# Two long-convolution stages: convolution taps of two tiles in turn, narrow sums in four column tiles, layer-norm statistics per token, other places for the z units

## The reference, cut to what matters

```python
def conformer_conv_mixer(h, w_in, conv_w, conv_b, ln_g, ln_b, w_out):
    proj = h @ w_in                                  # 1024 -> 3 x 2048
    val, glu_gate, z = jnp.split(proj, 3, axis=-1)
    u = val * jax.nn.sigmoid(glu_gate)
    u = causal_depthwise_conv(u, conv_w) + conv_b    # 31 taps per channel
    u = jax.nn.silu(layer_norm(u, ln_g, ln_b))       # over the 2048 channels
    return (u * jax.nn.silu(z)) @ w_out              # 2048 -> 1024
```

## Time and profile before

| | us |
|---|---|
| three runs | 1513.99, 1516.18, 1511.05 (median 1513.99) |
| profiled execution | 1511.99 |
| its span in the profile | 1510.0 |
| PE busy | 1485.9 |
| DVE, ACT, POOL busy | 1044.5, 828.2, 500.1 |

### The profile page before, as it was taken

One profiled execution on the slowest core, in us unless ns is written; L12 is line 12 of the kernel. 1 busy time (PEld: TensorE's weight loads), 2 busy tenths in 40 slices (PEclk: granted clock), 3 DMA queues, 4 the chain that ended last, 5 costly groups with the idle time before them and its releaser, 6 DMA issues.

```text
span 1510.0 us, 26643 instructions
## 1 busy us (share of the span) xinstructions
PE 1485.9 (98%) x10179; PEld 1372.2 (91%) x10179; DVE 1044.5 (69%) x2139; ACT 828.2 (55%) x1522; POOL 500.1 (33%) x459
## 2 busy tenths in 40 slices
PE   8999999999999999999999999999999999999999
PEld 6888899998899999999988888989888878999987
DVE  6899967455777786666599997666247667775532
ACT  4576656445665544444456676555336655555442
POOL 2687643433334200000057785154421112000033
PEclk9999999999999999999999999999999999999999
DMA  7554365666654568866444444654843223576653
GB/s 216 146 153 140 123 197 168 222 172 152 128 151 154 153 189 208 209 179 195 141 140 140 140 140 158 192 142 131 214 153 95 74 84 113 168 206 185 169 187 118
DMA packets 308114, 239.49 MB, mean 159 GB/s; under 512 B 18017, under 2 KB 286707, under 8 KB 307988
## 3 DMA queue, kind: packets, MB, share of 16 engines
q1 hardware_dynamic: 295816, 228.70, 52.0%
q10 hardware_dynamic: 12172, 9.10, 2.6%
HBM read 236.02 MB, written 1.75 MB: 157 GB/s over the span
## 4 chain that ended last, share of the span: by engine, by line
PE 80%; DVE 13%; ACT 3%; DMA 1%; issue 1%; POOL 1%; SPq 0%; DVEq 0%; ACTq 0%; POOLq 0%
PE bank L782 16%; PE bank L784 8%; PE bank L785 7%; PE bank L786 7%; PE bank L835 3%; DVE bank L1117 3%; PE bank L837 3%; PE bank L836 3%; PE bank L1633 3%; PE bank L1635 3%; PE bank L1634 3%; PE bank L1260 2%; DVE wlo L379 2%; PE bank L798 2%; PE bank L761 1%; PE bank L762 1%
## 5 line engine op out<-in xcount | busy, mean ns | idle before, releaser
L379 POOL TENSOR_TENSOR wlo<-ring,whi 128x1024 fp32r<-128x1024 f32 x101 | 252.5, 2507 | 852.1 <-ACT whi L370 852.1
L370 ACT CAST whi<-ring 128x1024 fp32r<-128x1024 f32 x330 | 339.3, 1046 | 228.0 <-PE bank L786 79.9
L379 DVE TENSOR_TENSOR wlo<-ring,whi 128x1024 fp32r<-128x1024 f32 (+1 forms) x229 | 294.1, 1294 | 186.9 <-ACT whi L370 185.9
L782 PE MATMUL bank<-sqb,ring 128*128 128x256 f32 x1504 | 330.3, 379 | 0.9 <-DMA ring<-in_a_w_in_dram 0.9
L782 PEld LDWEIGHTS bank<-sqb,ring 128*128 128x128 f32 x1504 | 285.4, 190 | 41.2 <-DMA ring<-in_a_w_in_dram 1.3
L784 PE MATMUL bank<-xh,whi 128*128 128x256 f32 x928 | 264.7, 285 | 1.5 <-DVE xl L707 1.5
L785 PE MATMUL bank<-xl,whi 128*128 128x256 f32 x928 | 263.2, 284 | 0.0
L786 PE MATMUL bank<-xh,wlo 128*128 128x256 f32 x928 | 263.1, 284 | 0.0
L1054 POOL TENSOR_TENSOR scratch<-scratch 128x256 f32<-128x256 f32 x288 | 200.3, 731 | 106.0 <-ACT scratch L999 95.3
L1117 DVE SCALAR_TENSOR_TENSOR bank<-scratch,convw,bank 128x256 f32<-128x256 f32 x576 | 231.1, 482 | 0.0
L784 PEld LDWEIGHTS bank<-xh,whi 128*128 128x128 f32 x928 | 178.7, 193 | 4.6 <-issue 3.5
(11 more groups left out here) (312 smaller groups left out, 2746.0 us busy)
## 6 DMA issues: line engine op xcount, KB each, us to landing
ring<-in_a_w_in_dram SPq DMA_DIRECT2D x64, 512.0 KB, 5.2
ring<-in_b_w_in_dram SPq DMA_DIRECT2D x32, 1024.0 KB, 6.0
ring<-in_c_w_in_dram SPq DMA_DIRECT2D x64, 512.0 KB, 5.4
ring<-in_w_in_dram SPq DMA_DIRECT2D x26, 1024.0 KB, 5.3
ring<-in_w_ffn_in_dram SPq DMA_DIRECT2D x44, 512.0 KB, 5.1
ring<-in_a_w_in_dram SPq DMA_DIRECT2D x16, 1024.0 KB, 5.2
ring<-in_a_w_out_dram SPq DMA_DIRECT2D x16, 1024.0 KB, 5.3
ring<-in_w_ffn_out_dram SPq DMA_DIRECT2D x10, 1024.0 KB, 5.0
```

The lines of the kernel that those rows point to most:

```text
L370: nc.scalar.copy(piece(whi, h)[:, :, 0:n], src).then_inc(hi_done, 1)
L379: engine.tensor_tensor(piece(wlo, h)[:, :, 0:n], src, piece(whi, h)[:, :, 0:n].bitcast(F32), ALU.subtract).then_inc(done, 1)
L782: mm = nc.tensor.matmul(o, halves[h][1][:, k, :], sqb[:, k, :], start=(k == 0), stop=(k == KD - 1))
```

## The change

- *Taps.* The tiles 3 to 14 are worked in pairs by DVE: one tap of the one, one tap of the other, each into one accumulator, so that one add a tile joins it with POOL's sum. Tiles 0, 1, 2 and 15 stay as they were. There are four buffers up instead of three. The gatings are at fixed steps of the pair, up to two tiles ahead; ACT's sigmoids are two tiles ahead, its squares two behind.
- *Sums.* Sums of two tiles and of their squares are four matmuls with one column of ones and 31 of zeros, into partitions 0 to 31, 32 to 63, 64 to 95 and 96 to 127 of bank 7.
- *Statistics.* The four sums are copied out, transposed so that tokens lie on partitions, reduced, and worked as 128x2 values. Two diagonal matrices, of the negative mean and of rstd, are spread over all partitions by a matmul with ones each. These PE steps lie inside z unit 6, after its first half's k = 1, 4 and 7. Mean and rstd are applied to two tiles at a time.
- *z units.* Three are in the loop, behind tiles 8, 12 and 14, five after it; unit 5 goes to bank 6.
- *Weight halves.* Output unit 0 is split at tile 10 and unit 1 at tile 15, and none further at these places.

```diff
+up = scratch[:, 0:4 * UPW].rearrange("p (r w) -> p r w", w=UPW)
+tmp = scratch[:, 1144:1144 + 4 * S].rearrange("p (r w) -> p r w", w=S)
+accp = scratch[:, 2168:2168 + 4 * S].rearrange("p (r a w) -> p r a w", a=2, w=S)
+csg = scratch[:, 3192:3192 + 2 * S].rearrange("p (r w) -> p r w", w=S)
+csq = scratch[:, 3704:3704 + 3 * S].rearrange("p (r w) -> p r w", w=S)
...
-        if c % 4 == 3:
-            z_group(c // 4)
-    for i in range(4, 8):
+        if c in (8, 12, 14):
+            z_group((8, 12, 14).index(c))
+    for i in range(3, 8):
...
+                if at_k and a == 0 and k in at_k:
+                    at_k[k]()
...
-Z_BESIDE = {6: 5, 10: 6, 13: 7}
-AHEAD_BESIDE = {8: 6, 13: 7}
-OUT_BESIDE = {13: 0, 15: 1}
+Z_BESIDE = {6: 5, 11: 6, 15: 7}
+OUT_BESIDE = {10: 0, 15: 1}
+TILE_GROUPS = [(0,), (1,), (2,)] + [(c, c + 1) for c in range(3, KE - 1, 2)] + [(KE - 1,)]
+SIGMOIDS = {0: (1,), 1: (2,), 2: (3, 4)} | {c: (c + 2,) for c in range(3, KE - 2)}
+SQUARES = {3: (0,), 4: (1, 2)} | {c: (c - 2,) for c in range(5, KE)}
+SUMS = {9: (0, 1), 11: (2,), 12: (3,), 14: (4,)}
+Z_BEHIND = {8: 0, 12: 1, 14: 2}
+one_column = cst[:, C_E1 + 15:C_E1 + 47]
+x_sums = rr[:, 0:S]
+l_sums = small[:, 208:212].rearrange("p (b s) -> p b s", b=TB)
+l_negm, l_msq, l_var, l_rstd = (small[:, 212 + 2 * i:214 + 2 * i] for i in range(4))
+l_warm = small[:, 220:221]
+l_diag = [tmp[:, 2 * i:2 * i + 2, :].rearrange("p r w -> p (r w)")[:, 0:S] for i in range(2)]
+stat_tr, stat_diag, stat_spread = sem("stat_tr"), sem("stat_diag"), sem("stat_spread")
 def z_bank(n, i):
-    return bank[2] if i < 4 else bank[n["z"][i][0] % 2]
+    return bank[2] if i < 3 else bank[6] if i == 5 else bank[n["z"][i][0] % 2]
...
-        wait(act, sqm_done, j * KE + c - 3)
-        nc.scalar.activation(sq4[:, c % 4, :], yb[:, c, :], ACT.Square).then_inc(sqd_done, 1)
+        wait(act, sqm_done, j * (KE // 2) + (c - 3) // 2 + 1 if c >= 3 else 0)
+        nc.scalar.activation(csq[:, c % 3, :], yb[:, c, :], ACT.Square).then_inc(sqd_done, 1)
     sigmoid(0)
     for c in range(KE):
         act.wait_ge(u_done, j * KE + c + 1)
         for i in range(TAPS_POOL):
             if i == TAPS_POOL // 3:
-                if c + 1 < KE:
-                    sigmoid(c + 1)
-                else:
-                    conf_z(act, n, 3)
-            if i == 2 * TAPS_POOL // 3 and c >= 3:
-                square(c - 3)
+                for s in SIGMOIDS.get(c, ())[0:1]:
+                    sigmoid(s)
+            if i == 2 * TAPS_POOL // 3:
+                for s in SIGMOIDS.get(c, ())[1:]:
+                    sigmoid(s)
+                for s in SQUARES.get(c, ()):
+                    square(s)
             k = TAPS_DVE + i
             m = (j * KE + c) * TAPS_POOL + i
             wait(act, tap_done, m - 3)
-            src = up[:, c % 3, k:k + S]
+            src = up[:, c % 4, k:k + S]
             bias = cols[:, ROWB + j * KE + c:ROWB + j * KE + c + 1] if i == 0 else 0.0
             nc.scalar.activation(tmp[:, m % 4, :], src, ACT.Identity, scale=taps[:, j, k, c:c + 1],
                                  bias=bias).then_inc(tmp_done, 1)
@@ -1003,11 +1018,15 @@
         if c == 2:
             act.wait_ge(m0_done, j + 1)
             nc.scalar.activation(shift, bank[6][:, 0:S], ACT.Copy, scale=-1.0 / P).then_inc(shift_done, 1)
-    for c in range(KE - 3, KE):
+    for i in range(2, 5):
+        conf_z(act, n, i)
+    for c in range(KE - 2, KE):
         square(c)
-    conf_z(act, n, 4)
+    nc.scalar.activation(l_warm, eps, ACT.Sqrt)
+    act.wait_ge(sqm_done, (j + 1) * (KE // 2))
+    nc.scalar.copy(x_sums, bank[7][:, 0:S]).then_inc(mean_done, 1)
     act.wait_ge(var_done, j + 1)
-    nc.scalar.activation(std[:, 0:S], std[:, 0:S], ACT.Sqrt, bias=eps).then_inc(lstd_done, 1)
+    nc.scalar.activation(l_var, l_var, ACT.Sqrt, bias=eps).then_inc(lstd_done, 1)
     for c in range(KE + 2):
         if c >= 2:
...
         if c in OUT_BESIDE:
-            act_ahead(act, n["out"][OUT_BESIDE[c]][2])
-        act.wait_ge(dn_done, j * KE + c + 1)
+            hi_to(act, last(n["out"][OUT_BESIDE[c]][2]))
+        act.wait_ge(dn_done, j * (KE // 2) + c // 2 + 1)
         lg = cols[:, ROWB + 32 + j * KE + c:ROWB + 32 + j * KE + c + 1]
         lb = cols[:, ROWB + 64 + j * KE + c:ROWB + 64 + j * KE + c + 1]
...
+    def join(gi):
+        cs = TILE_GROUPS[gi]
+        for a, c in enumerate(cs):
+            done = raw_done if c < 3 else conv_done
+            dve.wait_ge(pool_sum, j * KE + c + 1)
+            dve.wait_ge(step, ended[gi][a])
+            if len(cs) == 2:
+                nc.vector.tensor_tensor(yb[:, c, :], acc[gi % 2][:, a, :], accp[:, c % 2, 0, :], ALU.add).then_inc(done, 1)
+                continue
+            chain(dve, nc.vector.tensor_tensor(yb[:, c, :], acc[gi % 2][:, 0, :], accp[:, c % 2, 0, :], ALU.add))
+            dve.wait_ge(step, ended[gi][1])
+            nc.vector.tensor_tensor(yb[:, c, :], acc[gi % 2][:, 1, :], yb[:, c, :], ALU.add).then_inc(done, 1)
+    def shifted(c):
+        dve.wait_ge(raw_done, 3 * j + c + 1)
+        nc.vector.tensor_tensor(yb[:, c, :], yb[:, c, :], shift, ALU.add).then_inc(conv_done, 1)
     gated(0)
     dve.wait_ge(rows_copied, 3)
...
+    for gi, cs in enumerate(TILE_GROUPS):
+        for c in cs:
             dve.wait_ge(u_done, j * KE + c + 1)
...
+        if gi >= 2:
+            c = TILE_GROUPS[gi - 2][-1]
+            dve.wait_ge(*((raw_done, 3 * j + c + 1) if c < 3 else (conv_done, j * KE + c + 1)))
+        pair = len(cs) == 2
+        to = acc[gi % 2]
+        prev = [None, None]
+        for i in range(TAPS_DVE * len(cs)):
+            a = i % 2
+            k, c = (i // 2, cs[a]) if pair else (i, cs[0])
+            if pair and i == 12:
+                join(gi - 1)
+                if c == 3:
+                    shifted(2)
+            if pair and i == 16 and cs[0] + 3 < KE:
+                gated(cs[0] + 2)
+            if pair and i == 34:
+                gated(cs[0] + 3 if cs[0] + 3 < KE else cs[0] + 2)
+            if c < 2 and i == (17, 13)[c]:
+                gated(c + 1)
+            if c == 2 and i == 7:
+                gated(3)
+            if c == KE - 1 and i == 8:
+                join(gi - 1)
+            src = up[:, c % 4, k:k + S]
+            w = taps[:, j, k, c:c + 1]
+            if prev[a] is None and c >= 3 and (pair or a == 1):
+                ins = nc.vector.scalar_tensor_tensor(to[:, a, :], src, w, shift, ALU.mult, ALU.add)
+            elif prev[a] is None:
+                ins = nc.vector.tensor_scalar(to[:, a, :], src, w, None, ALU.mult)
+            else:
+                dve.wait_ge(step, prev[a])
+                ins = nc.vector.scalar_tensor_tensor(to[:, a, :], src, w, to[:, a, :], ALU.mult, ALU.add)
+            steps[0] += 1
+            ins.then_inc(step, 1)
+            prev[a] = steps[0]
+        ended[gi] = prev
+        if gi in (1, 2):
+            if gi == 2:
+                gated(4)
+            join(gi - 1)
+        if gi == 2:
             dve.wait_ge(shift_done, j + 1)
...
+            shifted(0)
+            shifted(1)
+    join(len(TILE_GROUPS) - 1)
+    dve.wait_ge(stat_tr, j + 1)
+    sums = bank[7][:, 0:S].rearrange("p (b s e r) -> p b s e r", b=TB, s=2, e=2)[:, :, :, :, 0]
+    chain(dve, nc.vector.tensor_reduce(l_sums, sums, AX, ALU.add))
+    chain(dve, nc.vector.tensor_scalar(l_negm, l_sums[:, :, 0], -1.0 / E, None, ALU.mult))
+    chain(dve, nc.vector.tensor_tensor(l_msq, l_negm, l_negm, ALU.mult))
+    nc.vector.scalar_tensor_tensor(l_var, l_sums[:, :, 1], 1.0 / E, l_msq, ALU.mult, ALU.subtract).then_inc(var_done, 1)
+    def diagonal(i, col):
+        for tb in range(TB):
+            nc.vector.tensor_scalar(l_diag[i][:, tb * P:(tb + 1) * P], ident, col[:, tb:tb + 1], None, ALU.mult).then_inc(stat_diag, 1)
+    diagonal(0, l_negm)
+    dve.wait_ge(lstd_done, j + 1)
+    chain(dve, nc.vector.reciprocal(l_rstd, l_var))
+    diagonal(1, l_rstd)
+    def both(b):
+        return bank[b][:, 0:S].unsqueeze(1).to_broadcast((P, 2, S))
+    def centre(q):
+        nc.vector.tensor_tensor(yb[:, 2 * q:2 * q + 2, :], yb[:, 2 * q:2 * q + 2, :], both(3), ALU.add).then_inc(dc_done, 1)
     dve.wait_ge(conv_done, j * KE + KE)
...
+    dve.wait_ge(stat_spread, 2 * j + 1)
+    for q in range(2):
+        centre(q)
+    dve.wait_ge(stat_spread, 2 * j + 2)
+    for q in range(KE // 2 + 2):
+        if q + 2 < KE // 2:
+            centre(q + 2)
+        if q < KE // 2:
+            dve.wait_ge(dc_done, j * (KE // 2) + q + 1)
+            nc.vector.tensor_tensor(yb[:, 2 * q:2 * q + 2, :], yb[:, 2 * q:2 * q + 2, :], both(2), ALU.mult).then_inc(dn_done, 1)
+        for c in (2 * q - 1, 2 * q):
+            if c in OUT_BESIDE:
+                lo_dve_to(dve, last(n["out"][OUT_BESIDE[c]][2]))
+        for c in (2 * q - 3, 2 * q - 2):
+            if 0 <= c < KE:
+                y_low(dve, n["y0"] + c, y_hi[:, c, :], y_lo[:, c, :])
     out_dve(dve, n)
 def conf_pe(pe, n):
@@ -1162,15 +1218,22 @@
```

(26 more changed lines are left out.)

120 lines of the change are left out of this document (13 added, 107 removed).

## The result

The changed kernel takes 1533.97 us (median), the kernel before on the same chip 1513.51: a ratio of 1.0144 with a 95% interval of 1.0127 to 1.016. It is slower by some 21 us, where 1510.0 was forecast and the range ended at 1517. Of its four runs one is slow (1629.39 us at a mean clock of 0.86) and isn't in the ratio; the other three lie between 1533.29 and 1534.42, which is the profiled one.

The account below looks back on a forecast made before the run. PE, busy 98% of the span with DVE neck and neck, was taken as the bound. Profiled 1512.0 us, minus 3.5 gained by output unit 1's earlier start in both stages, plus 1.5 for the clock, gave 1510.0; range 1501 to 1517.

Parts of the forecast that it names:

- Small edits at nothing: Extra pad memset, ACT's squares and moved gatings lie beside full PE or in waits, so they cost nothing.
- The groups wait for the gating two tiles back, which is early everywhere: First loop: PE never waits for a gating; closest at tile 8, wanted at 70.7, gating 6 done at 69.3.
- rival 2: Pair sums: four column tiles run one after the other, 1.84 us each, +6 us a stage, 1524 us; chance 14%.
- rival 3: Pair sums: column tiles run in twos, 0.98 us each, +0.9 us a stage, 1514 to 1515 us; chance 6%.
- rival 4: Statistics: an ACT table switch costs more than its load, 2.6 us more on each stage, 1515 us; chance 4%.
- the list of signs: Trace signs of right or wrong; wrong included PE waiting inside the loop for a gating, excluded by only 1.4 us.
- DVE's stretch beside POOL's split: Layer norm: DVE's low half of y took 1.92 us instead of 0.41; stretching puts unit 1 at 201.2, not 200.1.
- the net PE work, 8.3 us a stage: Sums and statistics: 13.8 us removed, 4.4 and 1.1 added, net 8.3 us a stage, 16.6 in all.
- The floor of 1495.4: Whole kernel: 1512.0 minus 16.6 us of PE work, if nothing else were late.
- 2.4 us of wait ahead of unit 0: Output projection: late weight splits make PE start unit 0 at 191.3 instead of 188.9, first stage, carried to the second.
- The clock was allowed 0.75 us a stage: Behind the second output-projection wait the clock may fall, losing 0 to 1.7 us a stage; 0.75 taken, together 1.5.
- Rival 1: Layer norm feeders keep up, unit 1 starts right behind unit 0: gain 4 to 5.5 us a stage, 1501 to 1504; 34%.

Follow-up runs that it names:

- experiment 1: Changed kernel with the pair sum of tiles 0 and 1 issued behind group 7 instead of group 9: 1519.81 us, ratio to the kernel before 1.0057.
- experiment 2: Changed kernel with a fourth place for the squares, PE's order left alone: 1520.72 us, ratio to the kernel before 1.0065.
- experiment 3: experiment 1 with pair sum 5 (tiles 10 and 11) moved from directly behind group 15 to behind z unit 3: 1514.86 us, ratio 1.0018.
- experiment 4: experiment 1 with the third z unit behind group 15 instead of group 14: 1510.72 us, ratio to the kernel before 0.9997.
- experiment 8: experiment 4 with weight splits at tiles 8 and 13, statistics one z unit earlier, first four output units' low halves all on DVE: 1500.36 us, ratio 0.9924.
- experiment 9: experiment 8 with three output units split, at tiles 8, 11 and 14, instead of two at 8 and 13: 1495.66 us, ratio 0.9895.

## Why the prediction was wrong

**What failed: a queue read without one of its waits.** Under "Small edits at nothing" the prediction put ACT's squares "beside full PE". The squares cost ACT little, but a square waits for two things, and I walked only one, the join of its tile. The other is the place of the square three tiles back, and in the changed kernel that is freed by an instruction of PE that had been moved to behind group 9. The square stands in the middle of ACT's taps, so all of ACT, POOL and DVE stand behind it. From this came "The groups wait for the gating two tiles back, which is early everywhere", which I had put down to the DVE walk alone: my closest margin, 1.4 us, was at tile 8, and group 8 indeed came through; the wait was at group 10, where gating 8 came 11 us late. Price: 7.2 us in each stage; experiments 1 and 2 got back 14.2 and 13.2 us of the 14.4.

**The same step again, smaller.** I let PE pass pair sum 5 directly behind group 15. Yet the prediction itself had the sigmoid of tile 15 wait some 6 us for that group (it was 6.06), and the square that pair sum 5 needs is behind that sigmoid. Price 5.7 and 3.3 us. Experiments 3 and 4 remove the wait in two ways: 4 is 9.1 us faster than experiment 1, 3 only 5.0.

**The sign of the rule I used.** That PE is the bound, and its feeders' edits therefore cost nothing, holds as long as no feeder waits for PE. A place that PE must free turns the cover around: PE came to the freeing instruction at 91.75 without a hole, and ACT had stood there since 80.15.

**Right, by its own steps.** Four column tiles of 32 run together: a pair sum takes 0.57 us from 114.24 to 114.81 (0.55 taken). With that row rivals 2 and 3 fall. The chain from the sigmoid of tile 15 to its POOL sum was 21.2 us (21.3), the way from the last pair sum to the first multiplication 5.7, a table switch one load of 1.28 and no more, which removes rival 4. These three were all the slower cases that had a price. The outcome was slower by a mechanism that had none; the list of signs named it (a wait for a gating inside the loop), but gave it no chance. Unit 1's start behind the first multiplication was 22.5 (21.3 to 22.4). DVE's stretch beside POOL's split was weighed as the reason; POOL's own queue, which experiment 8 shows to hold the row as well, was not.

**Mis-sized: the net PE work, 8.3 us a stage.** The four matmuls of a pair sum take 0.57 us, but the groups around them lose a little too. In the changed kernel, at a clock of 1.00:

```profile
114.81 14.08 PE L783 MATMUL bank<-sqb,ring 128*128 128x256 f32 x64
128.81 0.41 PE L1226 MATMUL bank<-wide,cst 128*32 128x256 f32 x2
...
129.38 20.99 PE L783 MATMUL bank<-sqb,ring 128*128 128x256 f32 x96
```

Two groups and one pair sum take 129.38 - 114.81 = 14.57 us, two groups 13.82: the pair sum costs 0.75. A full sum costs its 0.43 and nothing beside it (in the kernel before two groups with one sum between them start at 57.30 and 64.64, and 7.34 is 6.91 + 0.43). Eight pair sums are 1.6 us dearer than taken, and a stage's net PE work is 6.7 us less and not 8.3 (7.0 with the wait in experiment 9). What makes these 0.19 us around a pair sum no run isolates. The floor of 1495.4 was too low for the same reason; that experiment 9 reaches it is due to PE's waits that went as well.

**Undersized: unit 0 of the second stage, and the clock.** I had 2.4 us of wait ahead of unit 0 in both stages; the changed kernel has 3.39 and, in the second, where POOL makes the first low half, 4.30:

```profile
951.86 0.43 PE L838 MATMUL bank<-y_hi,whi 128*128 128x256 f32 x1 [4.30 <-issue]
```

In the table of the result that matters little, since unit 1 is late anyway. The clock was allowed 0.75 us a stage. In the changed kernel it took 2.8 and 2.6 us in the first loop alone, part of the two prices above; in experiment 4, without the rings, it took about 1.7 behind each of the first stage's two waits. And of the 1.5 us of waits that were to go from the first output projection, the kernel before has one of 0.73, ahead of 216.97.

**Rival 1** (the feeders keep up, 1501 to 1504) was no outcome of this change. Experiment 8, where no wait in the projections is longer than 0.9 us, takes 1500.4, near its price; with five edits more it is no test of it.
